# Second layer's expansion: the upper weights meet both parts of the tokens in one product of 512 columns

## The reference, cut to what matters

```
hm = rmsnorm(x, g_pre_mlp) * (1 + sc2) + sh2
x = x + ga2 * rmsnorm(square(relu(hm @ w_mlp1)) @ w_mlp2, g_post_mlp)
```

## Time and profile before

| | us |
|---|---|
| median of three runs | 1422.7 |
| profiled execution | 1422.65 |
| its span | 1420.8 |
| TensorE busy | 1383.6 |
| VectorE busy | 999.6 |
| ScalarE busy | 674.1 |
| GpSimd busy | 83.4 |

### The profile page before, as it was taken

The page is one execution under the profiler, slowest core; times in us unless marked ns, Lnnn a source line. Parts: engine busy times, 40 slices in busy tenths (PEclk is TensorE's granted clock), DMA queues, the critical chain, the costliest instruction groups (busy, mean ns, idle before and its releaser), DMA issues.

```text
span 1420.8 us, 21794 instructions
## 1 busy us (share of the span) xinstructions
PE 1383.6 (97%) x8606; PEld 1191.9 (84%) x8606; DVE 999.6 (70%) x1512; ACT 674.1 (47%) x1059; POOL 83.4 (6%) x125
## 2 busy tenths in 40 slices
PE   6999999999999999999999999999999999999997
PEld 3787767898888888889867899888998999899996
DVE  3777677676876857679785765577996546786867
ACT  4422366651331314465266644466545664654544
POOL 0000000010001111100000450000000000000000
PEclk9999999999999999999999999999999999999999
DMA  9422460443635548346313555555444434455453
GB/s 385 187 71 85 178 239 30 149 163 119 249 136 222 207 164 309 134 147 213 119 46 119 178 178 187 202 200 193 167 164 178 163 120 177 149 179 193 163 208 119
DMA packets 39510, 241.06 MB, mean 170 GB/s; under 512 B 4496, under 2 KB 4928, under 8 KB 15488
## 3 DMA queue, kind: packets, MB, share of 16 engines
q1 hardware_dynamic: 28624, 198.92, 38.4%
q0 software_dynamic: 10800, 40.92, 8.3%
HBM read 238.75 MB, written 1.07 MB: 169 GB/s over the span
## 4 chain that ended last, share of the span: by engine, by line
PE 88%; DVE 4%; ACT 4%; DMA 2%; issue 1%; SPq 0%; DVEq 0%; ACTq 0%
PE ps L708 45%; PE ps L758 18%; PE ps L791 5%; PE ps L675 2%; PE ps L728 2%; PE ps L820 2%; DMA w<-in_stream 1%; PE ps L849 1%; PE ps L1089 1%; PE ps L1262 1%; ACT w_hi L488 1%; PE ps L904 1%; DMA U<-in_start 1%; PE ps L1246 1%; DVE w_lo L498 1%
## 5 line engine op out<-in xcount | busy, mean ns | idle before, releaser
L498 DVE TENSOR_TENSOR w_lo<-w,w_hi 128x1024 fp32r<-128x1024 f32 x332 | 393.2, 1228 | 73.7 <-ACT w_hi L488 69.6
L708 PE MATMUL ps<-h_hi,w_hi 128*128 128x256 f32 (+1 forms) x1488 | 443.6, 312 | 1.3 <-DVE h_lo L2935 0.9
L488 ACT ACTIVATE w_hi<-w 128x1024 fp32r<-128x1024 f32 x332 | 333.0, 1053 | 225.3 <-DMA w<-in_stream 225.1
L708 PE MATMUL ps<-h_lo,w_hi 128*128 128x256 f32 (+1 forms) x1488 | 439.6, 309 | 0.0
L708 PE MATMUL ps<-h_hi,w_lo 128*128 128x256 f32 (+1 forms) x1488 | 356.7, 309 | 0.0
L708 PEld LDWEIGHTS ps<-h_hi,w_hi 128*128 128x128 f32 x1488 | 283.7, 191 | 17.9 <-issue 2.0
L708 PEld LDWEIGHTS ps<-h_lo,w_hi 128*128 128x128 f32 x1488 | 283.9, 191 | 15.0 <-issue 0.5
L708 PEld LDWEIGHTS ps<-h_hi,w_lo 128*128 128x128 f32 x1488 | 249.9, 191 | 14.4
L758 PE MATMUL ps<-w_hi,g_hi 128*128 128x512 f32 x344 | 134.7, 391 | 2.3 <-DVE g_lo L2969 1.0
L758 PE MATMUL ps<-w_hi,g_lo 128*128 128x512 f32 x344 | 134.0, 389 | 0.0
L758 PE MATMUL ps<-w_lo,g_hi 128*128 128x512 f32 x344 | 120.9, 389 | 0.0
(11 more groups left out here) (362 smaller groups left out, 1959.3 us busy)
## 6 DMA issues: line engine op xcount, KB each, us to landing
w<-in_stream SPq DMA_DIRECT2D x176, 1024.0 KB, 4.8
hf<-in_mod_blocks POOLq DMA_DIRECT2D x38, 512.0 KB, 4.1
SW<-in_mod_blocks POOLq DMA_DIRECT2D x18, 512.0 KB, 4.9
U<-in_start SPq DMA_DIRECT2D x4, 1024.0 KB, 16.0
GA<-gates POOLq DMA_DIRECT2D x6, 512.0 KB, 4.4
w<-in_start SPq DMA_DIRECT2D x2, 1024.0 KB, 9.7
w<-in_stream SPq DMA_DIRECT2D x4, 512.0 KB, 7.4
GA<-in_start SPq DMA_DIRECT2D x2, 1024.0 KB, 10.9
```

The source lines that it names most:

```text
L488: act.activation(k.w_hi[:, c.slot, half], k.w[:, c.slot, half], ACT.Copy).then_inc(k.hi_done, 1)
L498: dve.tensor_tensor(k.w_lo[:, c.slot, half], k.w[:, c.slot, half], k.w_hi[:, c.slot, half].bitcast(f32), ALU.subtract).then_inc(k.lo_done, 1)
L708: last = pe.matmul(k.banks(2 * c.pair, n, j * (512 if tiles == 2 else n)), w[a][:, c.slot, at:at + 128], h[b][:, kt * stride:kt * stride + n],
```

## The change

In layer 2 the chunks of the expansion, but for the pair computed ahead, go through a new function, `to_features_wide`. Upper and lower tokens now lie in one tensor, `h_both`, of two parts 4096 columns apart. The upper weights meet both parts of 256 tokens in one product of 512 columns, which fills a whole bank: upper tokens' sums in its first half, lower tokens' in its second. The lower weights meet the upper tokens in a product of 256 columns, into the first half. So the hidden feature's sum is now the first half plus the second. ScalarE copies the second halves of both banks to the rear of `R`, VectorE adds them to the first halves in PSUM and writes `R`, and ScalarE does Relu and Square there. VectorE's sum counts as a read of the chunk (`dve_read`). The memory of `hs` and `h_lo` keeps its place.

```diff
+            add(("mlp", l), ["up"] * 2 + ["up_wide"] * 2 + ["down"] * 4)
+            kinds.extend((["up_wide"] * 4 + ["down"] * 4) * (GROUPS1 - 1))
...
-        self.h_hi = sb("h_hi", [128, KT * NT_ALL], f32r)
...
-        self.h_lo = sb("h_lo", [128, KT * NT_ALL], f32r)
+        self.h_both = sb("h_both", [128, 2, KT * NT_ALL], f32r)
+        self.h_hi, self.h_lo = self.h_both[:, 0, :], self.h_both[:, 1, :]
...
+def to_features_wide(k, pe, c, h, middle=None, waits=True):
+    if waits:
+        chunk_waits(k, pe, c)
+    for j in range(2):
+        bank = 2 * c.pair + j
+        steps = [(kt, "hi") for kt in range(KT)] + [(kt, "lo") for kt in range(KT)]
+        for kt, w in steps if j == 0 else [(kt, w) for kt in range(KT) for w in ("hi", "lo")]:
+            if j == 0 and kt in (0, 4):
+                (hi_wait if w == "hi" else half_wait)(k, pe, c, kt // 4)
+            at, tok = kt * 256 + j * 128, kt * NT_ALL
+            if w == "hi":
+                pe.matmul(k.banks(bank, 2 * SEQ).rearrange("p (a n) -> p a n", a=2), k.w_hi[:, c.slot, at:at + 128],
+                          k.h_both[:, :, tok:tok + SEQ], start=kt == 0, stop=False)
+            else:
+                last = pe.matmul(k.banks(bank, SEQ), k.w_lo[:, c.slot, at:at + 128], h["hi"][:, tok:tok + SEQ],
+                                 start=False, stop=kt == KT - 1)
+        if j == 0 and middle:
+            middle()
+    last.then_inc(k.chunk_mm, 1)
...
+            if l == 1 and not paired:
+                act.wait_ge(k.chunk_mm, c.value(lambda m: m + 1))
+                act.activation(k.R[:, j % 2, 2 * n:4 * n].rearrange("p (t n) -> p t n", t=2),
+                               k.ps[:, 2 * c.pair:2 * c.pair + 2, n:2 * n], ACT.Copy).then_inc(k.act_read, 1)
+                act.wait_ge(k.dve_read, c.value(lambda m: DVE_READ_COUNT[m]))
+                act.activation(k.R[:, j % 2, 0:2 * n], k.R[:, j % 2, 0:2 * n], ACT.Relu).then_inc(k.s("squared"), 1)
+                k.wait(act, "squared", l, squared_count(l, i, j) - 1)
...
+    def sums(c, j):
+        dve.wait_ge(k.act_read, c.value(lambda m: ACT_READ_COUNT[m]))
+        upper, lower = (k.R[:, j % 2, at:at + 2 * SEQ].rearrange("p (t n) -> p t n", t=2) for at in (0, 2 * SEQ))
+        dve.tensor_tensor(upper, k.two(c, SEQ), lower, ALU.add).then_inc(k.dve_read, 1)
...
                 feed_lo(k, dve, at(j + 2))
+                if l == 1:
+                    sums(at(j), j)
```

More of the change, by code:

```diff
@@ L190, in chunk_kinds @@
         add(("out", l), ["out"] * 4)
-        add(("mlp", l), (["up"] * 4 + ["down"] * 4) * GROUPS1)
+        if l == 0:
+            add(("mlp", l), (["up"] * 4 + ["down"] * 4) * GROUPS1)
+        else:
+            add(("mlp", l), ["up"] * 2 + ["up_wide"] * 2 + ["down"] * 4)
+            kinds.extend((["up_wide"] * 4 + ["down"] * 4) * (GROUPS1 - 1))
     add("proj2", ["va_low", "va", "qa", "qa", "ka", "ka"] + ["qb"] * 6 + ["kb"] * 6 + ["vb_low", "vb"] * 3)
@@ L201 @@
 N_CHUNKS = len(KINDS)
-ACT_READS = {"qa", "ka", "cf_a", "cf_g", "kv", "q", "nk", "nq", "nv", "sc_x", "sc_b", "up", "va", "vb", "gate", "up_gate",
+ACT_READS = {"qa", "ka", "cf_a", "cf_g", "kv", "q", "nk", "nq", "nv", "sc_x", "sc_b", "up", "up_wide", "va", "vb", "gate", "up_gate",
              "up_val"}
-DVE_READS = {"cf_a", "kv", "q", "nk", "nq", "nv", "sc_x", "sc_c", "sc_b", "out", "down", "qa", "ka",
+DVE_READS = {"up_wide", "cf_a", "kv", "q", "nk", "nq", "nv", "sc_x", "sc_c", "sc_b", "out", "down", "qa", "ka",
              "va", "qb", "kb", "vb", "a_out", "b_out", "mix", "up_gate", "up_val", "down2"}
@@ L381, in __init__ @@
         self.Y_parts = sb("Y_parts", [128, 4 * D], f32r)
-        self.h_hi = sb("h_hi", [128, KT * NT_ALL], f32r)
         scratch = ExitStack()
+        sb("before_hs", [128, KT * NT_ALL], f32, scratch)
         self.hs = sb("hs", [128, KT * NT_ALL], f32, scratch)
         scratch.close()
-        self.h_lo = sb("h_lo", [128, KT * NT_ALL], f32r)
+        self.h_both = sb("h_both", [128, 2, KT * NT_ALL], f32r)
+        self.h_hi, self.h_lo = self.h_both[:, 0, :], self.h_both[:, 1, :]
         gates = ExitStack()
@@ L474, in run_loop, with squared_count @@
     return eng.Fori(0, times)
+def squared_count(l, i, j):
+    if l == 0:
+        return i * 4 + j + 1
+    if isinstance(i, int) and i == 0:
+        return (1, 2, 4, 6)[j]
+    return i * 8 + 2 * j
 def feed_hi(k, act, c, halves=(0, 1)):
@@ L1331, in group @@
         for j in range(2 if first else 0, 4):
+            if l == 1:
+                to_features_wide(k, pe, at(j), h, waits=(first, j) != (True, 2),
+                                 middle=(lambda: pair_turned(k, pe)) if (first, j) == (True, 2) else None)
+                continue
             to_features(k, pe, at(j), h, KT, 256, 2, n, NT_ALL,
-                        waits=(l, first, j) != (1, True, 2),
-                        middle=(lambda: pair_turned(k, pe)) if (l, first, j) == (1, True, 2) else
-                        (lambda: pe_mod_step(k, pe, MLP_TURNS[j - 1], 4)) if last and l == 0 and j in (1, 2) else None)
+                        middle=(lambda: pe_mod_step(k, pe, MLP_TURNS[j - 1], 4)) if last and l == 0 and j in (1, 2) else None)
         k.wait(pe, "hidden", l, i * 4 + 3)
@@ L1976, in group @@
                 act_mod_step(k, act, MLP_TURNS[j - 1], 4)
-            if paired:
-                act.wait_ge(k.s("first_mm"), 2)
-            else:
[L1980 to L1986, removed]
+            if l == 1 and not paired:
[5 more added lines that the diff above has]
+                k.wait(act, "squared", l, squared_count(l, i, j) - 1)
+            else:
+                if paired:
+                    act.wait_ge(k.s("first_mm"), 2)
+                else:
+                    act.wait_ge(k.chunk_mm, c.value(lambda m: m + 1))
+                if j >= 2:
+                    k.wait(act, "hidden", l, i * 4 + (j - 1))
+                act.activation(k.R[:, j % 2, 0:2 * n].rearrange("p (t n) -> p t n", t=2),
+                               k.ps[:, 4 + 2 * j:6 + 2 * j, 0:n] if paired else k.two(c, n),
+                               ACT.Relu).then_inc(k.act_read, 1)
+                act.wait_ge(k.act_read, c.value(lambda m: ACT_READ_COUNT[m]))
             act.activation(k.R[:, j % 2, 0:2 * n], k.R[:, j % 2, 0:2 * n],
@@ L2762, in group @@
                 feed_lo(k, dve, at(j + 2))
-            k.wait(dve, "squared", l, i * 4 + (j + 1))
+                if l == 1:
+                    sums(at(j), j)
+            k.wait(dve, "squared", l, squared_count(l, i, j))
             r, cols = k.R[:, j % 2, 0:2 * n], 2 * j * n
```

## The result

In twenty runs of each kernel on one chip the changed kernel took 1424.52 us (median; 1423.55 to 1428.34), the kernel before 1422.28: **2.24 us more**, a ratio of 1.0016 with a 95% interval of 1.001 to 1.0022. That is a real loss, but well inside the 0.3% within which the prediction counted the time as unchanged. The profiled execution took 1424.68 us, its span 1422.9. Where positions of two runs are compared, they are counted from the start of the 26 products ahead of the second layer's MLP (782.85 before, 782.77 after), so that what earlier stages do by chance drops out.

The account below looks back on a forecast made before the run. The prediction took TensorE, busy 97% of the span, to bound the kernel. Its terms, -2.89 + 0.91 + 1.82 + 0.72 = +0.56 us on 1422.65, gave 1423.2 us, with an 8-in-10 range of 1420.3 to 1426.5.

Parts of the forecast that it names:

- likeliest case: The forecast itself, all four terms summed to +0.56 us, with its own range 1422.2 to 1424.5 us; chance 0.55.
- TensorE's saving: Expansion chunks of layer 2's MLP: 5.55 us instead of 5.76, 0.206 saved in each of fourteen, -2.89 us.
- First group: First contraction: TensorE waits for hidden values because VectorE's sum stands behind its split, +0.91 us.
- Last group: Last contraction: TensorE waits for hidden values delayed by ScalarE's table loads and the splits, +1.82 us.
- Tail: After the last contraction's start: ScalarE's next upper split waits for its own late work, not its load, +0.72 us.
- A: Rival: the whole saving stays because the waits at the first and last contraction are hidden, 1419.8 us; chance 0.15.
- B: Rival: the wide product saves nothing, taking 240 ns, so expansion chunks keep 5.76 us, 1425.2 us; chance 0.15.
- C: Rival: reading the moving operand in two pieces slows every wide product, 1430.6 us at 45 ns more each; chance 0.05.
- D: Rival: VectorE's turn overruns a chunk, so waits come in groups two and three too, 1426.1 us; chance 0.10.

Follow-up runs that it names:

- e4: Changed kernel with all eight wide products ahead of the eight narrow ones in the second tile of a chunk too; 1424.21 us.
- e7: Changed kernel with VectorE taking the chunk's sum first and its lower split in two halves, around the hidden values; 1421.94 us.
- e6: Changed kernel with the last group's Sin and Exp, and VectorE's small sum for the Exp, ahead of that group's first chunk; 1421.95 us.
- e5: Changed kernel with 4 instructions more on each of VectorE and ScalarE, waits long met, behind the last chunk's hidden values; 1423.90 us.
- e10: Changed kernel with Sin and Exp early, wide products first in both tiles, sum first in the first group only, 4 instructions more on VectorE; 1419.65 us.
- e11: As e10, but the 4 instructions more are on ScalarE and none on VectorE; 1420.75 us.
- e9: Changed kernel with each wide product again two of 256 columns, all else kept, lower tokens' sums misplaced, for timing only; 1426.25 us.
- e3: Changed kernel with the last group's Sin and Exp moved behind the fourth chunk's Square; 1427.05 us.

## Why the prediction was nearly right, step by step

The time, 1424.5, lay in the range and at the very edge of the likeliest case's own (1422.2 to 1424.5). That it did is in part luck: the terms' sum was forecast at +0.56 and came out at +0.98 at the last write, TensorE's saving was a quarter too large, and 1.15 us, half of the whole difference, is a term that the forecast did not have.

- **TensorE's saving, -2.89: mis-sized, -2.13** (14 chunks of 0.152). 227 and 120 ns held for products in a row (8 wide in 1.82, 8 narrow in 0.95). A chunk still took 5.605 us, as wide and narrow products by turns take more than the two rows' sum:

```profile
832.67 0.40 PE L746 MATMUL ps<-h_both,w_hi 128*128 128x512 f32 x1
832.91 0.28 PE L749 MATMUL ps<-h_both,w_lo 128*128 128x256 f32 x1
833.02 0.40 PE L746 MATMUL ps<-h_both,w_hi 128*128 128x512 f32 x1
```

  A pair takes 0.354 us on average over a tile, not 0.347. e4 removes a part of it. I had taken spacings from streams of one size and added them.
- **First group, +0.91: +0.89, by two errors that cancel.** Counted from the 26 products, the contraction starts 0.78 us later than in e7, where TensorE does not wait (18.92 against 18.14); starting again costs 0.11 more, which the forecast did not have. The path to the hidden values was right to 0.1 us (start 801.69, forecast 801.79); TensorE itself came later than forecast, by the saving that its two chunks did not make, so the wait was shorter by 0.1.
- **Last group, +1.82: +1.71** (start 153.31 from the 26 products; 151.60 in e6, which has the first wait and not this one). The path was right: 18.3 us from the end of the first chunk. TensorE came later by what its three chunks did not save (0.16), so it waited less. Starting again costs nothing here, since the chain stays with VectorE, which goes straight on to its next split (936.03). e6 and e7 show both causes, the table loads and the place behind the split.
- **Tail, +0.72: +0.72.** The upper split 11.59 us behind the contraction's first product, as forecast. -0.15 is given back in later stages, where the wait named under e5 shrinks. With it the measured terms add up to +1.04, for +0.98.
- **Missing: +1.15** for the late part of the last write. I read nothing behind the last instruction and took the write's landing as fixed. e5, e10 and e11 show it. It belongs to the length of VectorE's program, and to the wide form only in so far as that form makes it 14 instructions longer.
- **Rivals.** A is wrong for this kernel, both waits were there. e10, a different kernel, reaches its time: 1419.65 against its 1419.8. B, that the wide product saves nothing, is wrong by e9. Its 1425.2 is near the time for another reason. For C no sign: wide products in a row take 227 ns. D is wrong: no wait in groups two and three, VectorE waits 1.36 us for each Square and ScalarE 0.76 or more for each sum.
- The Trainium skill's gap of N/2.4 plus 2.5 ns (TensorE: Matmul & The Clock Gate, Back-to-back issue gap), which that section gives for an isolated product, does not hold here either: by it a wide and a narrow product by turns would take 325 ns, an estimate; the trace has 354.

## What to carry to other kernels

Here, work moved from a bound engine to idle ones was free in the steady state and was paid at the edges, in the first and the last group, where those engines have other jobs. So lay the edge out instruction by instruction, with what queues behind each. Before moving a job into an idle stretch, name who waits for what stands behind it (e3 against e6). And when a difference of one microsecond matters, compare the last landing too, not only the last instruction.

## What the runs showed of the hardware

- Where a load of 8 KB of VectorE's code fell under the last write of the output, that write's last part landed 1.15 to 1.17 us late: in six of the eleven experiments and the changed kernel, and in no run without such a load. Four instructions more on VectorE moved the load away, and the median was 1.1 us shorter (e10 against e11). How the load holds the part up is not shown.
- A wide and a narrow product by turns take 7 ns a pair more than they do in rows (354 for 347), and a tile of eight wide and then eight narrow ones about 0.02 us more than its products (2.79 for 2.77).
- After a wait of 0.69 or 1.54 us TensorE's second product comes 0.34 us behind the first instead of 0.23.
- A moving operand in two pieces of 256 columns, 4096 apart, costs nothing that shows: its products in a row stand 227 ns apart, as those with one piece of 512 do.
